# The last banks of pool, attention and two feed-forward layers finished by token tile, with the norm of tile 0 ahead of tile 1's statistics

## The chip, the core and the metric

The kernel runs on one core of a Trainium2 chip. Five engines work side by side, each with its own queue, and wait for each other by semaphores: TensorE (PE in the rows; PEld is its weight load), VectorE (DVE), ScalarE (ACT), GpSimd (POOL) and SyncE (SP, which here only issues transfers). The metric is the device time of one execution in microseconds.

## What is computed

The reference runs two blocks, one after the other, on a sequence of 256 tokens with 1024 features. The first has two mixers (mLSTM, gated linear attention), each followed by a mixture of 16 experts. The second, in which the change lies, is:

```python
def second_block(x, ...):
    for i in range(DEPTH):                       # 2
        if i % 2 == 0:
            h = _multiscale_pool(x, pool_w[j], pool_scale[j])
        else:
            h = _diff_attention(x, w_qkv[j], w_o[j], ...)
        x = _layernorm(ALPHA_2 * x + h, ln_mix_g[i], ln_mix_b[i])
        x = _layernorm(ALPHA_2 * x + _swiglu(x, w_gate[i], w_up[i], w_down[i]), ...)
    return x
```

So there are four layers, each closed by a layer norm: pool, feed-forward 0, attention, feed-forward 1. `_swiglu` is `(silu(x @ w_gate) * (x @ w_up)) @ w_down` with 2816 hidden features. The norm takes mean and variance over the 1024 features of a token. Everything is float32.

## The kernel before

Tokens lie in two tiles of 128 (i = 0, 1), features in two halves of 512 (c = 0, 1). The sum of a layer and its residual is gathered in four banks of the accumulation memory: `acc(i, c)` is bank 4 + 2i + c, so banks 4 and 5 are tile 0 and banks 6 and 7 are tile 1.

**Splits.** A product of the big layers is three matmuls on halves of a float32 number. For each chunk of weights ScalarE writes the high part (`w_hi`, line 563) and VectorE the rest (`w_lo`, line 568). TensorE waits for the rest by `split_ready`, and ScalarE may only write the next high part into a buffer when `chunk_done` says that TensorE is through with the chunk that lay there. `chunk_done` counts chunks, and TensorE raises it with the last matmul of a chunk.

**Feed-forward** (`ffn_tensor`). `down(s, at, units, base, end)` adds two chunks f = 0, 1 of the last product: for each f it waits for `split_ready` and for the hidden values (`fh_ready`), then runs banks 4, 5, 6, 7 with three matmuls each (line 1642). The last call has `end=True`. The high part of its chunk 1 can only be written when the chunk ahead in that buffer is done.

**Attention** (`att_tensor`). The output product runs over chunks 24 to 31 (`out_chunk`, matmuls at line 613). An even chunk adds to half 0 of both tiles (banks 4 and 6), an odd one to half 1 (banks 5 and 7). Its splits go through three buffers.

**Pool** (`pool_tensor`). Sixteen matmuls at line 1540, by group g of features and then by tile, so that the banks are finished in the order 4, 6, 5, 7.

**The norm.** `ln_statistics` (VectorE) waits for the banks in the order of `acc_waits`, takes `bn_stats` of each (line 331) and `bn_aggr` of a tile (line 334). ScalarE takes the root (`ln_scalar`, line 350), VectorE the reciprocal `rstd` and `nmr` (lines 323, 324), and then ScalarE writes half 0 of the normed rows `y` (line 353) and VectorE half 1 (line 344). TensorE transposes `y` (`transpose_x`, line 409), ScalarE scales it into `xT` (line 421), and VectorE splits that (lines 458, 460) for the next layer's matmuls. Ahead of each `transpose_x` but the first, `keep_clock(0, 10)` runs ten products of the identity with itself (line 392), whose results nobody reads. The last norm is `final_vector` (lines 369, 371), whose rows go out by four transfers of SyncE.

**What stands between on the queues.** Each queue is in order. At the end of feed-forward 0 and of attention ScalarE has first the high part of the next layer's chunk 0, which waits for `chunk_done` of all but the last chunk, then the table load and the roots of the norm. VectorE takes the rest of the next layer's chunks 0 and 1 right behind the last rows `y`, ahead of the split of `xT`.

## Time and profile before

| | us |
|---|---|
| median of three runs | 1791.68 |
| lowest, highest | 1790.61, 1797.0 |
| the profiled execution | 1799.73 |
| its span, first to last instruction | 1798.0 |
| TensorE busy in it | 1417.8 |
| VectorE busy | 600.7 |
| ScalarE busy | 426.8 |

The experts take the stretches up to about 1250 us, in which the core moves some 424 GB/s of weights. What the change touches lies behind that: the pool ends at 1274 us, feed-forward 0 at 1471 us, attention at 1591 us and feed-forward 1 at 1788 us of the span. Of a row of the timeline the first number is the start in us from the span's start, the second how long it took; a bracket at its end is the engine's idle time before it and what ended that. A row may hold several instructions (x8).

### The profile page before, as it was taken

Reading aid. Unit: us, or ns where it says so; the run is one execution under the profiler, and the core shown is the slowest. Engines: PE = TensorE matmul, PEld = TensorE weight load, DVE = VectorE, ACT = ScalarE, POOL = GpSimd, SP = SyncE. Lnnn points to the kernel's source line nnn. Section 1 sums busy time; section 2 is a strip of 40 time slices with the busy share of each in tenths; the row PEclk is TensorE's granted clock in tenths of the full one; section 3 lists DMA queues with packets and bytes.
Section 4 is the critical chain, followed back from the end, with each engine's and each line's share of the span. In section 5 each row is a group of like instructions: output and inputs, shape, how many; then the busy total and the mean of one; then the engine's idle time right before and its main releaser. Section 6 shows DMA issues by size and latency. Waiting matters only on the chain.

```text
span 1798.0 us, 21119 instructions
## 1 busy us (share of the span) xinstructions
PE 1417.8 (79%) x8842; PEld 914.0 (51%) x8842; DVE 600.7 (33%) x988; ACT 426.8 (24%) x671; POOL 39.5 (2%) x47
## 2 busy tenths in 40 slices
PE   7999765576575689987665655757999999999997
PEld 6787221121121275672211211212999989889996
DVE  5555100000000147651000000001555566865556
ACT  3442000000000143430000000001434454653443
POOL 3000000000000002100000000000000000000000
PEclk9988978787687889999776887877999999999999
DMA  9736999999999952369999999999365665226560
GB/s 338 215 115 262 379 423 424 423 424 425 423 424 424 397 202 94 128 270 392 424 424 424 424 424 424 424 424 395 131 201 186 211 219 179 71 94 193 183 207 23
DMA packets 145635, 533.47 MB, mean 297 GB/s; under 512 B 9740, under 2 KB 73500, under 8 KB 96284
## 3 DMA queue, kind: packets, MB, share of 16 engines
q1 hardware_dynamic: 142948, 527.07, 74.7%
q10 hardware_dynamic: 1176, 2.18, 0.8%
q0 software_dynamic: 1440, 3.18, 0.6%
q8 instruction: 55, 0.90, 0.2%
q14 instruction: 16, 0.13, 0.0%
HBM read 529.78 MB, written 2.62 MB: 296 GB/s over the span
## 4 chain that ended last, share of the span: by engine, by line
PE 52%; DMA 35%; DVE 5%; SPq 4%; ACT 2%; issue 1%; POOL 0%; DVEq 0%; ACTq 0%; POOLq 0%
PE bank L1626 14%; PE bank L613 11%; DMA moe_slots<-in_moe_w_up 7%; DMA arena<-in_moe_w_up 7%; PE bank L1642 7%; PE bank L1104 5%; DMA ring<-in_moe_w_down 4%; DMA ring<-in_moe_w_up 4%; SPq L1270 4%; DMA xT<-in_moe_w_down 3%; DMA moe_slots<-in_moe_w_down 3%; DMA xT<-in_moe_w_up 3%; PE bank L497 3%; PE bank L1143 3%; PE bank L1085 2%; DMA h_slot<-in_moe_w_up 2%
## 5 line engine op out<-in xcount | busy, mean ns | idle before, releaser
L568 DVE TENSOR_TENSOR w_lo<-ring,w_hi 128x1024 fp32r<-128x1024 f32 x200 | 244.3, 1224 | 238.0 <-ACT w_hi L563 230.9
L1104 PE MATMUL bank<-ring,arena 128*32 128x512 f32 x1016 | 214.9, 731 | 100.3 <-DMA ring<-in_moe_w_up 41.2
L563 ACT ACTIVATE w_hi<-ring 128x1024 fp32r<-128x1024 f32 x200 | 211.1, 1058 | 313.0 <-PE bank L1626 151.3
L1143 PE MATMUL bank<-ring,arena 128*32 128x512 f32 x536 | 158.2, 931 | 82.9 <-DMA arena<-in_moe_w_down 24.5
L1626 PE MATMUL bank<-xT_hi,w_hi 128*128 128x256 f32 x704 | 199.8, 284 | 0.6 <-DVE xT_lo L460 0.4
L1626 PE MATMUL bank<-xT_hi,w_lo 128*128 128x256 f32 x704 | 199.2, 283 | 0.0
L1626 PE MATMUL bank<-xT_lo,w_hi 128*128 128x256 f32 x704 | 199.2, 283 | 0.0
L1237 DVE TENSOR_TENSOR arena<-arena,bank 64x512 f32<-64x512 f32 x32 | 22.1, 691 | 450.1 <-ACT arena L1177 450.1
L1104 PEld LDWEIGHTS bank<-ring,arena 128*32 128x32 f32 x1016 | 46.9, 122 | 223.5 <-issue 206.3
L1626 PEld LDWEIGHTS bank<-xT_hi,w_hi 128*128 128x128 f32 x704 | 135.0, 192 | 1.6 <-issue 0.9
L1626 PEld LDWEIGHTS bank<-xT_lo,w_hi 128*128 128x128 f32 x704 | 135.1, 192 | 0.7
L1626 PEld LDWEIGHTS bank<-xT_hi,w_lo 128*128 128x128 f32 x704 | 135.1, 192 | 0.0
L1177 ACT ACTIVATE arena<-bank 64x512 f32<-64x512 f32 x32 | 18.8, 588 | 463.0 <-PE bank L1104 463.0
L1104 PE MATMUL bank<-arena 128*32 128x512 f32 x448 | 98.4, 697 | 36.3 <-DMA ring<-in_moe_w_up 23.1
L1143 PEld LDWEIGHTS bank<-ring,arena 128*32 128x32 f32 x536 | 36.9, 162 | 170.7 <-issue 170.7
L1243 DVE COPY arena<-bank 128x512 f32<-128x512 f32 x8 | 5.5, 691 | 326.4 <-PE bank L1143 326.4
L1104 PE MATMUL bank<-moe_slots,arena 128*32 128x512 f32 x384 | 87.9, 741 | 33.6 <-DMA xT<-in_moe_w_up 18.6
L1143 PE MATMUL bank<-arena 128*32 128x512 f32 x192 | 72.9, 934 | 28.5 <-DMA ring<-in_moe_w_down 28.5
L1143 PE MATMUL bank<-moe_slots,arena 128*32 128x512 f32 x192 | 72.5, 916 | 26.4 <-DMA xT<-in_moe_w_down 26.4
L1184 ACT ACTIVATE arena<-bank 128x512 f32<-128x512 f32 x8 | 4.8, 597 | 345.7 <-PE bank L1143 345.7
L613 PE MATMUL bank<-w_hi,xT_hi 128*128 128x512 f32 x176 | 70.5, 400 | 5.2 <-DVE xT_lo L460 4.2
L1642 PE MATMUL bank<-w_hi,h_hi 128*128 128x512 f32 x176 | 70.4, 400 | 0.0
(286 smaller groups left out, 2282.9 us busy)
## 6 DMA issues: line engine op xcount, KB each, us to landing
ring<-in_moe_w_gate SPq DMA_DIRECT2D x76, 1024.0 KB, 26.4
ring<-in_moe_w_down SPq DMA_DIRECT2D x67, 1024.0 KB, 27.1
ring<-in_moe_w_up SPq DMA_DIRECT2D x51, 1024.0 KB, 26.7
arena<-in_moe_w_up SPq DMA_DIRECT2D x28, 1024.0 KB, 26.8
arena<-in_moe_w_gate SPq DMA_DIRECT2D x28, 1024.0 KB, 26.5
moe_slots<-in_moe_w_up SPq DMA_DIRECT2D x24, 1024.0 KB, 27.1
moe_slots<-in_moe_w_gate SPq DMA_DIRECT2D x24, 1024.0 KB, 26.5
moe_slots<-in_moe_w_down SPq DMA_DIRECT2D x24, 1024.0 KB, 27.0
```

The lines of the kernel that those rows point to most:

```text
L497: last = nc.tensor.matmul(ps[bank][:, :], xT3[:, kk, i * P:(i + 1) * P], w[:, k, :], start=(kk == 0), stop=(kk == KD - 1))
L563: nc.scalar.activation(dst, raw, ACT.Copy).then_inc(hi_ready, 1)
L568: nc.vector.tensor_tensor(lo, raw, hi.bitcast(F32), ALU.subtract).then_inc(split_ready, 1)
L613: last = nc.tensor.matmul(dst, *(ops if weights_first else ops[::-1]), start=(start and p == 0), stop=(stop and p == 2))
L1085: last = nc.tensor.matmul(ps[B_GA[k // 4]][:, (k % 4) * P:(k % 4 + 1) * P], pair_cols(y3[:, i, :], k), pick[:, i, :], start=(i == 0), stop ...
L1104: last = nc.tensor.matmul(ps[B_GU[j % 2]][32 * c:32 * c + 32, :], xin[:, k, j * CAP:(j + 1) * CAP], w, start=(k == 0), stop=(k == KD - 1), ...
L1143: last = nc.tensor.matmul(ps[B_DN[c]][32 * j:32 * j + 32, :], hT[:, j // 2, at:at + CAP], slot(ud[j], 2)[:, f % 2, c * HALF:(c + 1) * HALF ...
L1177: nc.scalar.activation(silu[64:128, j % 2, :], ps[B_GU[j % 2]][0:64, :], ACT.Silu).then_inc(silu_ready, 1)
L1237: nc.vector.tensor_tensor(hmid[64 * (j % 2):64 * (j % 2) + 64, j // 2, :], silu[64:128, j % 2, :], ps[B_GU[j % 2]][64:128, :], ALU.mult).t ...
L1270: sp.dma_start(slots[u.slot], src[:, q, :]).then_inc(slot_landed[u.slot], 16)
L1626: last = nc.tensor.matmul(ps[2 * s + f][:, n * SEQ:(n + 1) * SEQ], w_parts[wp][:, buf, k * P:(k + 1) * P], (xT_hi3, xT_lo3)[xp][:, k, :], ...
L1642: last = nc.tensor.matmul(acc(i, c), h_parts[hp][:, 2 * s + f, i * P:(i + 1) * P], w_parts[wp][:, f, c * HALF:(c + 1) * HALF], start=False ...
```

## The change

`TILE_FIRST = (4, 5, 6, 7)` names the four norms of the second block. For these:

- TensorE ends with tile 0 first. The pool loops over tiles outside and groups inside. The last `down` of a feed-forward runs tile 0 of chunk 0, tile 0 of chunk 1, and then tile 1 of both; the waits for both chunks stand ahead of tile 1, and `chunk_done` of both is raised in tile 1's part. Attention runs tile 0 of chunks 30 and 31, then tile 1 of both, and raises `chunk_done` with tile 1 as well.
- VectorE takes tile 0's reciprocal and rows ahead of the wait for bank 7, where before it took the reciprocal there and the rows behind bank 7's statistics.
- `transpose_x` has no identity products ahead of tile 0's transposes and seven between tile 0's and tile 1's.

```diff
+        TILE_FIRST = (4, 5, 6, 7)
+        def xhat(dve, n, i):
+            dve.wait_ge(rstd_ready, NT * n + i + 1)
+            nc.vector.tensor_scalar(y3[:, i, HALF:D], acc(i, 1), rstd[:, i:i + 1], nmr[:, i:i + 1],
+                                    ALU.mult, ALU.add).then_inc(xhat_vec, 1)
...
             for at, (i, c, done, count) in enumerate(acc_waits()[n]):
+                if at == 3 and n in TILE_FIRST:
+                    inverse_std(0)
+                    rows(0)
                 dve.wait_ge(done, count)
-                if at == 3:
+                if at == 3 and n not in TILE_FIRST:
                     inverse_std(0)
...
         def transpose_x(pe, gen):
-            if gen:
+            if gen and gen - 1 not in TILE_FIRST:
                 keep_clock(0, 10)
...
+                elif i and gen - 1 in TILE_FIRST:
+                    keep_clock(0, 7, P)
...
-            for g in range(4):
-                for i in range(NT):
+            for i in range(NT):
+                for g in range(4):
...
+            def down_tile(s, f, i, units, end):
+                for c in range(2):
+                    for p, (wp, hp) in enumerate(PARTS):
+                        last = nc.tensor.matmul(acc(i, c), ...)
+                if i == NT - 1:
+                    last.then_inc(chunk_done, 1)
...
                 for f in range(2):
                     pe.wait_ge(split_ready, at + (f + 1))
                     pe.wait_ge(fh_ready, base + (f + 1))
+                    for i in range(1 if end else NT):
+                        down_tile(s, f, i, units, end)
+                if end:
+                    for f in range(2):
+                        down_tile(s, f, 1, units, end)
...
-            for c in range(29, 32):
-                att_mix.out_chunk(pe, c)
+            att_mix.out_chunk(pe, 29)
+            for i in range(NT):
+                for c in (30, 31):
+                    att_mix.out_chunk(pe, c, (i,))
```

TensorE, the last two chunks of a feed-forward, before: from the middle of chunk 0 to the middle of chunk 1 (line 1642; a wait in brackets).

```order
L1642 MATMUL bank5<-w_lo,h_hi 128x512
L1642 MATMUL bank6<-w_hi,h_hi 128x512
L1642 MATMUL bank6<-w_hi,h_lo 128x512
L1642 MATMUL bank6<-w_lo,h_hi 128x512
L1642 MATMUL bank7<-w_hi,h_hi 128x512
L1642 MATMUL bank7<-w_hi,h_lo 128x512
L1642 MATMUL bank7<-w_lo,h_hi 128x512
L1642 MATMUL bank4<-w_hi,h_hi 128x512 [waits fh_ready,split_ready]
```

The same place now (the matmul has moved to line 1652).

```order
L1652 MATMUL bank4<-w_hi,h_hi 128x512 [waits fh_ready,split_ready]
L1652 MATMUL bank4<-w_hi,h_lo 128x512
L1652 MATMUL bank4<-w_lo,h_hi 128x512
L1652 MATMUL bank5<-w_hi,h_hi 128x512
L1652 MATMUL bank5<-w_hi,h_lo 128x512
L1652 MATMUL bank5<-w_lo,h_hi 128x512
L1652 MATMUL bank4<-w_hi,h_hi 128x512 [waits fh_ready,split_ready]
```

The six matmuls on banks 6 and 7 that stood ahead of the second wait now stand behind it, after the six on banks 4 and 5 of chunk 1.

VectorE, the norm after attention, before.

```order
L331 BN_STATS stats<-bank4 128x6 [waits chunk_done]
L331 BN_STATS stats<-bank6 128x6 [waits chunk_done]
L331 BN_STATS stats<-bank5 128x6 [waits acc_done]
L334 BN_AGGR mv<-stats 128x2 [waits vec_chain]
L323 RECIPROCAL rstd<-std 128x1 [waits std_ready,chunk_done]
L324 SCALAR_TENSOR_TENSOR nmr<-mv,rstd 128x1 [waits vec_chain]
L331 BN_STATS stats<-bank7 128x6
L334 BN_AGGR mv<-stats 128x2 [waits vec_chain]
L344 TENSOR_SCALAR y<-bank5,rstd,nmr 128x512 [waits rstd_ready]
L323 RECIPROCAL rstd<-std 128x1 [waits std_ready]
```

And now.

```order
L341 BN_STATS stats<-bank4 128x6 [waits acc_done]
L341 BN_STATS stats<-bank5 128x6 [waits acc_done]
L344 BN_AGGR mv<-stats 128x2 [waits vec_chain]
L341 BN_STATS stats<-bank6 128x6 [waits chunk_done]
L330 RECIPROCAL rstd<-std 128x1 [waits std_ready]
L331 SCALAR_TENSOR_TENSOR nmr<-mv,rstd 128x1 [waits vec_chain]
L322 TENSOR_SCALAR y<-bank5,rstd,nmr 128x512 [waits rstd_ready]
L341 BN_STATS stats<-bank7 128x6 [waits chunk_done]
L344 BN_AGGR mv<-stats 128x2 [waits vec_chain]
L330 RECIPROCAL rstd<-std 128x1 [waits std_ready]
```

Tile 0's rows have moved ahead of bank 7's statistics, and the second reciprocal now stands right behind the second aggregate, where before the rows of tile 0 lay between them.

## Rows read from the trace of the kernel before

**Rows 1.** The page's TensorE clock in 40 slices of the span, tenths of full speed.

```profile
PEclk9988978787687889999776887877999999999999
```

**Rows 2.** Busy time of stretches: PE, PEld, DVE, ACT, POOL; granted clock; DMA share, GB/s.

```profile
668.20:670.50 2.30, 0.00 (x0) 0.00 (x0) 1.03 (x1) 2.28 (x4) 0.00 (x0) 1.00 0.75 290
671.00:674.40 3.40, 3.40 (x16) 2.99 (x15) 3.37 (x6) 0.70 (x1) 0.00 (x0) 0.51 0.02 5
1475.10:1477.40 2.30, 0.00 (x0) 0.01 (x1) 2.27 (x4) 2.30 (x6) 0.00 (x0) 1.00 0.00 0
1477.50:1483.00 5.50, 5.50 (x25) 4.52 (x26) 4.95 (x8) 4.30 (x6) 0.00 (x0) 1.00 0.18 52
```

**Rows 3.** The timeline where the pool ends: start us, us, engine, line, operation.

```profile
1266.62 7.07 PE L1540 MATMUL bank<-ring,arena 128*128 128x256 f32 x32
...
1272.87 0.70 DVE L331 BATCH_NORM_STATS2 stats<-bank 128x6 f32<-128x512 f32 x1 [1.89 <-PE bank L1540]
...
1273.60 0.21 DVE L334 BATCH_NORM_AGGREGATE mv<-stats 128x2 f32<-128x12 f32 x1
...
1274.24 0.16 DVE L323 RECIPROCAL rstd<-std 128x1 f32<-128x1 f32 x1 [0.43 <-ACT std L350]
...
1276.04 0.15 DVE L323 RECIPROCAL rstd<-std 128x1 f32<-128x1 f32 x1
...
1276.42 0.78 ACT L353 ACTIVATE y<-bank,nmr,rstd 128x512 f32<-128x512 f32 x1 [0.65 <-DVE nmr L324]
...
1277.25 1.09 PE L409 MATMUL bank<-cst,y 128*128 128x128 f32 x8 [0.42 <-ACT y L353]
```

**Rows 4.** The timeline where feed-forward 0 ends.

```profile
1465.17 0.39 PE L1642 MATMUL bank<-w_hi,h_hi 128*128 128x512 f32 x1
...
1466.52 1.23 DVE L568 TENSOR_TENSOR w_lo<-ring,w_hi 128x1024 fp32r<-128x1024 f32 x1 [0.48 <-ACT w_hi L563]
...
1467.92 0.40 PE L1642 MATMUL bank<-w_hi,h_hi 128*128 128x512 f32 x1
...
1468.18 1.06 ACT L563 ACTIVATE w_hi<-ring 128x1024 fp32r<-128x1024 f32 x1 [1.69 <-PE bank L1642]
...
1469.26 1.28 ACT L350 ACT_TABLE_LOAD   x1
...
1470.43 0.40 PE L1642 MATMUL bank<-w_lo,h_hi 128*128 128x512 f32 x1
...
1470.55 0.30 ACT L350 ACTIVATE std<-mv,cst 128x1 f32<-128x1 f32 x1
1470.66 2.40 PE L392 MATMUL bank<-cst 128*128 128x128 f32 x20
...
1473.13 0.81 DVE L344 TENSOR_SCALAR y<-bank,rstd,nmr 128x512 f32<-128x512 f32 x1
...
1473.86 2.35 DVE L568 TENSOR_TENSOR w_lo<-ring,w_hi 128x1024 fp32r<-128x1024 f32 x2
...
1477.42 0.47 PE L613 MATMUL bank<-w_hi,xT_hi 128*128 128x512 f32 x1 [2.36 <-DVE xT_lo L460]
```

**Rows 5.** The timeline where attention ends.

```profile
1588.01 2.06 DVE L331 BATCH_NORM_STATS2 stats<-bank 128x6 f32<-128x512 f32 x3 [2.35 <-PE bank L613]
...
1588.07 1.06 ACT L563 ACTIVATE w_hi<-ring 128x1024 fp32r<-128x1024 f32 x1 [3.85 <-PE bank L613]
...
1590.45 0.30 ACT L350 ACTIVATE std<-mv,cst 128x1 f32<-128x1 f32 x1
...
1593.03 0.81 DVE L344 TENSOR_SCALAR y<-bank,rstd,nmr 128x512 f32<-128x512 f32 x1
```

**Rows 6.** The timeline where feed-forward 1, and with it the kernel, ends.

```profile
1783.78 1.23 DVE L568 TENSOR_TENSOR w_lo<-ring,w_hi 128x1024 fp32r<-128x1024 f32 x1 [0.50 <-ACT w_hi L563]
...
1787.71 0.39 PE L1642 MATMUL bank<-w_lo,h_hi 128*128 128x512 f32 x1
...
1794.80 0.75 DVE L371 SCALAR_TENSOR_TENSOR arena<-y,rstd,arena 128x512 f32<-128x512 f32 x1
```

More of the change, by code:

```diff
@@ L359, in final_vector, with rows @@
         def final_vector(dve, link, n):
-            inverse_std = ln_statistics(dve, link, n)
-            dve.wait_ge(gb_in, 32)
-            for i in range(NT):
-                if i:
-                    inverse_std(i)
+            def rows(i):
+                if i == 0:
+                    dve.wait_ge(gb_in, 32)
                 dve.wait_ge(rstd_ready, NT * n + i + 1)
@@ L603, in lo, with products @@
                     split_lo(dve, self.raw(c), self.buffer(c), self.at + c)
-            def products(self, pe, c, todo, operand):
+            def products(self, pe, c, todo, operand, more=False):
                 pe.wait_ge(split_ready, self.at + c + 1)
@@ L1536, in pool_tensor @@
             w = slots[u.slot].rearrange("p (g k n) -> p g k n", g=4, k=2)
-            for g in range(4):
-                for i in range(NT):
+            for i in range(NT):
+                for g in range(4):
                     for k in range(2):
@@ L1632, in gate_up @@
                         last.then_inc(chunk_done, 1)
+            def down_tile(s, f, i, units, end):
+                for c in range(2):
+                    for p, (wp, hp) in enumerate(PARTS):
+                        last = nc.tensor.matmul(acc(i, c), h_parts[hp][:, 2 * s + f, i * P:(i + 1) * P],
+                                                w_parts[wp][:, f, c * HALF:(c + 1) * HALF],
+                                                start=False, stop=(end and f == 1 and p == 2))
+                        if f == 1 and i == 0 and c == 0 and p == 0:
+                            last.then_inc(unit_done, units)
+                        if end and f == 1 and p == 2 and (i, c) != (1, 1):
+                            last.then_inc(acc_done, 1)
+                if i == NT - 1:
+                    last.then_inc(chunk_done, 1)
             def down(s, at, units, base, end=False):
@@ L1804, in out_chunk @@
                                        False, 2 * b + k2 == KD - 1, False)
-                                      for i in range(NT) for k2 in range(2)], ("z", 2))
+                                      for i in tiles for k2 in range(2)], ("z", 2), more=tiles == (0,))
         att_mix = HeadMixer(att_u, 4, chunk0["att"])
```

41 lines of the change are left out of this document (16 added, 25 removed).

## Prediction

> **What bounds the kernel now.** I read the chain of work that ended last first: it is half TensorE, a third transfers, and the transfers all belong to the experts, ahead of 1250 us. From there on the chain runs over TensorE inside a layer and hands over at each norm to VectorE and ScalarE and back. So an edit at a layer's end counts one for one if it moves the first matmul of the next layer. The granted clock tells the same: it changes again and again in the first 28 slices and stands near full in the last twelve [rows 1]. Then I read the timeline at the four ends. After the pool the order is: last matmul, bank 7's statistics, rows of tile 1 at 1276.42, tile 1's transposes at 1277.25 [rows 3]. After feed-forward 0 it is: last matmul at 1470.43, rows of tile 1 at 1473.13, two rests `w_lo` for the next layer on VectorE, the split of `xT`, first product at 1477.42 [rows 4]. Attention ends in the same way, and there ScalarE is late as well: it waits for a chunk until 1588.07, then loads a table, and its root of tile 0 at 1590.45 is what VectorE's reciprocal waits for [rows 5]. The last norm ends with VectorE at 1795.55 (1794.80 + 0.75), and the rest of the span is a transfer [rows 6].
>
> The reader should see that tile 1's rows, not tile 0's, release the next layer everywhere. Doing tile 0 earlier helps only where it takes work out of the way between the last bank and tile 1's rows.
>
> **What an end costs in steps.** From bank statistics to the aggregate are 0.73 us (1272.87 to 1273.60), from there over ScalarE's root to the reciprocal 0.64 (to 1274.24), from a reciprocal to its rows 0.38 (1276.04 to 1276.42) [rows 3]. With the new order bank 7 reaches tile 1's rows in 0.73 + 0.64 + 0.38 = 1.75 us. Before, the root of tile 1 ran under tile 0's rows; now the round over ScalarE (0.64, where VectorE waits) lies open.
>
> **Pool: 0.65 us gained.** The 32 records of line 1540 take 7.07 us [rows 3], so each of the 16 matmuls takes 0.44. By tile, bank 6 is done after twelve, at 1271.9, and bank 7 after sixteen, at 1273.7 as before. Statistics of bank 6 at 1272.0, reciprocal at 1272.65 (tile 0's root is long there), tile 0's rows at 1273.05, so VectorE is free when bank 7 ends at 1273.75. Tile 1's rows start 1.75 later, at 1275.5, where before it was 1276.42: 0.9 earlier. TensorE: tile 0's transposes go at 1273.9 and take 1.1 [rows 3]; seven identity products are 14 records, and 20 take 2.40, so 1.6 us [rows 4]; tile 1's transposes start at 1276.6 and not at 1276.35, against 1277.25 before. Gain 0.65; bounds 0 (the rest hides it) and 0.9 (the identity products hide).
>
> **Feed-forward 0: 3.35 us lost.** Two waits that were covered are laid open. *The first is TensorE's.* Before, chunk 0's twelve matmuls started at 1465.17 and chunk 1's at 1467.92, 0.23 each, and the rest of chunk 1 was ready at 1466.52 + 1.23 = 1467.75 [rows 4]: just in time, with no slack. Now TensorE has six matmuls of tile 0 to do, is through at 1466.5 and waits until 1467.8. VectorE's rest follows ScalarE's high part, and that waits for the chunk ahead in the buffer, so nothing brings it forward. Tile 0's banks end when they did before; tile 1's twelve matmuls follow, the last at 1471.8 where it was 1470.43: 1.37 late. *The second is ScalarE's.* Its high part for the next layer waits for `chunk_done` of chunk 0, which was raised at the end of the first twelve (ScalarE at 1468.18) and is now raised six matmuls into tile 1's part, at 1470.8. Queued behind it are the table load and tile 0's root: 1470.9 + 1.08 + 1.29 puts the root at 1473.27, where it was 1470.55 [rows 4]. VectorE stands behind that root with the reciprocal, and behind the reciprocal stands bank 7. Reciprocal at 1473.65, tile 0's rows at 1474.05, bank 7's statistics 0.68 later at 1474.73 (the bank has been done since 1472.2, its last matmul's start and 0.4), tile 1's rows 1.75 later, at 1476.48: 3.35 after 1473.13. The two rests and the split follow on VectorE as before [rows 4], so the first product moves to 1480.8. Bounds: 1.4, if only TensorE's wait counted, and 3.5.
>
> **Attention: 2.0 us lost.** Here TensorE doesn't wait and ends when it did. But chunk 30 is through after 18 of the last 24 matmuls and not after 12, six times 0.23 = 1.36 later, so ScalarE's high part moves from 1588.07 to 1589.43 and the root from 1590.45 to 1591.8 [rows 5]. Reciprocal 1592.2, tile 0's rows 1592.6, bank 7's statistics 1593.27, tile 1's rows 1595.0, against 1593.03: 2.0, of which 1.36 is the high part and the rest the open round over ScalarE. Bounds 0.6 and 2.1. A transfer that SyncE may now issue one matmul group earlier gives nothing, since its reader ScalarE comes later.
>
> **Feed-forward 1: 1.85 us lost.** TensorE waits again, until 1783.78 + 1.23 = 1785.01 [rows 6], and ends 1.37 later. No high part stands ahead of the root, which is ready early. Its last matmul starts at 1787.71 + 1.37 = 1789.1, bank 6's last three before that and is done 0.4 after its start, at 1788.8, and VectorE waits for it: statistics 1788.8, reciprocal 1789.4, rows from 1789.8, four operations of 0.75 each [rows 6], a little overlapped, in 2.9, bank 7's statistics at 1792.7, then 0.73, 0.64 and 0.38, and four operations in 3.0: end at 1797.4, against 1795.55. Bounds 1.2 and 2.0.
>
> Sum: -0.65 + 3.35 + 2.0 + 1.85 = **+6.55 us**.
>
> **The clock.** Without identity products ahead of tile 0's transposes TensorE now stands still for 2.7 us after feed-forward 0 (1472.2 to 1474.9) and after attention (1590.7 to 1593.4); before, the products filled that. The rows show both outcomes for a still stretch of this size: after 2.3 us without a matmul at 668 us the granted clock was 0.51 in the next 3.4 us, after 2.3 us at 1475 us it stayed 1.00 [rows 2]. I counted eleven still stretches of 2.2 to 2.8 us that began at full clock, of which one of each kind stands in the rows; six were followed by a fall, so each of the two has about an even chance, and it may differ from run to run. A fall makes TensorE's 2.7 us of transposes and identity products take up to twice as long, 1.5 to 2.7 more; VectorE's two rests (2.3 us) hide some 0.3 to 0.8 of it. I take 1.3 us for a fall, with 0 and 3 as bounds (3 if it reaches the first products).
>
> The Trainium skill (TensorE: Matmul & The Clock Gate, "What's actually happening") says that the throttled state is the default and that activity releases it; that speaks against taking the identity products away, and by it both places fall and the time would be 1791.7 + 6.55 + 2.6 = 1800.8. The trace agrees only half, by the two stretches of [rows 2].
>
> **Rivals.** *Both falls or a long one.* Clock 0.5 after both ends, or into the first products: 6.55 + 2.6 to 6 = 9 to 12.5 us, 1801 to 1804. For it speaks the row at 671 us, against it the one at 1475 us [rows 2].
> *Faster: the waits don't bite.* The norm gives 0.65 after the pool and, since bank 7's way is 1.75 us and not 2.3, some 0.5 after each of feed-forward 0 and attention, 1.7 in all: 1790.0. It decides at the rest of the last chunk: it needs `w_lo` by 1466.5, and the trace has 1467.75, right when TensorE came for it; and it needs ScalarE's high part not to be last, where the trace has it ahead of the root at both ends [rows 4, 5]. So it has little behind it.
> *Half of it hides.* The late ends are met by slack that I don't see, for instance if the first layers' matmuls wait for something else anyway, or if the high part is in time: 1 to 5 us, 1792.7 to 1796.7. Against it: after feed-forward 0 the first product starts as soon as the split is there.
>
> **Numbers.** The profiled execution took 1799.73 us, 8.05 above the median, with the experts' transfers ahead of 1250 us in it; the edits lie behind and carry over to the median as differences. Likeliest is the sum with one fall, 6.55 + 1.3 = 7.85: 1791.68 + 7.85 = **1799.5 us** (1807.6 for an execution like the profiled one). Chances: the sum with none or one fall 0.58, both or a long fall 0.25, half hidden 0.12, faster 0.05. The range goes from 1795.5 (half hidden at its upper end) to 1803.0 (most of the long falls). About 0.5%, 9.0 us, is what a measurement of this kernel can tell from no change; my 7.85 is 0.44%, just inside it. Both falls or a long one, and the upper end of the first case, lie beyond it: slower 0.33, same 0.65, faster 0.02.
>
> **What would show it.** In the changed kernel's trace: a still TensorE of 1.3 us between the sixth and seventh of the last 24 matmuls of each feed-forward; tile 0's root 2.7 us later against the last matmul's old place after feed-forward 0, 1.4 later after attention; VectorE idle for 0.4 us between the second aggregate and reciprocal at all four; tile 1's rows 1.75 us after bank 7's statistics; after the pool first transposes of tile 1 0.65 earlier. Wrong would be: a rest of the last chunk that comes earlier than 1.3 us after TensorE is through with tile 0, or a root ahead of bank 6.

## The result, and the profile after

The changed kernel took **1801.71 us** (median of 8 runs, 1798.78 to 1803.77) and the kernel before 1792.51 (8 runs, 1790.61 to 1800.0): a ratio of **1.0042**, 95% interval 1.0025 to 1.0059. That is the ratio of the means, 1801.57 and 1794.05, so the loss is 7.5 us, with 4.5 to 10.6 us as its interval; the medians differ by 9.2. The forecast was 1799.5 us, 7.85 us lost. The ratios of the experiments are not the quotients of the medians beside them either. The profiled execution of after took 1803.34 us, its span 1801.6.

What lies ahead of the pool differs from one execution to the next: the pool's first matmul starts between 1258.1 and 1266.6 us of the span in the fourteen traces of this study, with nothing changed ahead of it. Small terms can't be read from the span or the time of one execution then. I count each station (a place in the program that every version passes) from the pool's first matmul and compare with the same distance in before. By that count the end of after is 7.85 us late, in one execution.

**The pool's end**, timeline of after; columns as in [rows 3].

```profile
1262.39 7.07 PE L1554 MATMUL bank<-ring,arena 128*128 128x256 f32 x32
...
1269.50 0.70 DVE L341 BATCH_NORM_STATS2 stats<-bank 128x6 f32<-128x512 f32 x1
...
1270.52 1.73 PE L403 MATMUL bank<-cst 128*128 128x128 f32 x14
1270.80 0.16 DVE L330 RECIPROCAL rstd<-std 128x1 f32<-128x1 f32 x1 [0.36 <-ACT std L358]
...
1271.19 0.78 ACT L361 ACTIVATE y<-bank,nmr,rstd 128x512 f32<-128x512 f32 x1 [0.42 <-DVE nmr L331]
...
1272.08 1.04 PE L422 MATMUL bank<-cst,y 128*128 128x128 f32 x8
```

Tile 1's rows start 8.80 us after the first matmul (1271.19 - 1262.39), where [rows 3] have 9.80 (1276.42 - 1266.62). The way from bank 7's statistics to the rows is 1.69 us, with VectorE idle for 0.36 behind ScalarE's root. Tile 1's transposes start 0.11 us after ScalarE has written the rows (1271.19 + 0.78), so the seven identity products in front of them cost next to nothing. Two things make up the gain. From bank 7's statistics to the rows before needs 1.91 us (1276.42 less the first row below), 0.22 more than now. And its statistics stood behind the reciprocal of tile 0, which waited for ScalarE's root: they start 7.89 us after the first matmul, now 7.11. Timeline of before, bank 7's statistics behind the pool, feed-forward 0 and attention, with attention's last matmul:

```profile
1274.51 0.69 DVE L331 BATCH_NORM_STATS2 stats<-bank 128x6 f32<-128x512 f32 x1
...
1471.22 0.69 DVE L331 BATCH_NORM_STATS2 stats<-bank 128x6 f32<-128x512 f32 x1
...
1590.31 0.40 PE L613 MATMUL bank<-w_lo,xT_hi 128*128 128x512 f32 x1
...
1591.12 0.69 DVE L331 BATCH_NORM_STATS2 stats<-bank 128x6 f32<-128x512 f32 x1
```

**Feed-forward 0's end**, timeline of after, to be laid beside [rows 4].

```profile
1462.62 0.50 PE L1652 MATMUL bank<-w_hi,h_hi 128*128 128x512 f32 x1 [1.09 <-DVE w_lo L581]
...
1465.73 1.06 ACT L576 ACTIVATE w_hi<-ring 128x1024 fp32r<-128x1024 f32 x1 [4.42 <-PE bank L1652]
...
1466.60 0.39 PE L1652 MATMUL bank<-w_lo,h_hi 128*128 128x512 f32 x1
1466.81 1.28 ACT L358 ACT_TABLE_LOAD   x1
1468.10 0.30 ACT L358 ACTIVATE std<-mv,cst 128x1 f32<-128x1 f32 x1
1468.43 0.16 DVE L330 RECIPROCAL rstd<-std 128x1 f32<-128x1 f32 x1 [1.38 <-ACT std L358]
...
1469.55 0.69 DVE L341 BATCH_NORM_STATS2 stats<-bank 128x6 f32<-128x512 f32 x1
...
1469.66 1.09 PE L422 MATMUL bank<-cst,y 128*128 128x128 f32 x8 [2.67 <-ACT y L361]
...
1471.24 0.81 DVE L322 TENSOR_SCALAR y<-bank,rstd,nmr 128x512 f32<-128x512 f32 x1
...
1475.52 0.76 PE L626 MATMUL bank<-w_hi,xT_hi 128*128 128x512 f32 x1 [2.33 <-DVE xT_lo L473]
```

The chain can be read downwards: TensorE has done its six matmuls of tile 0 and waits 1.09 us for the rest of the last chunk (first row), ScalarE has waited 4.42 us for a bank before it may write the next layer's high part, then come the table load and the root, VectorE's reciprocal has waited 1.38 us for that root, and TensorE stands still for 2.67 us until ScalarE has written tile 0's rows. The page "ScalarE: Activation LUTs" of the Trainium skill (section "What ACT_TABLE_LOAD costs") has 1283 ns for the load, as the row shows, and a drain of 1380 ns on top; here the root starts 0.01 us behind the load, so the row decides and a switch costs this queue 1.3 us.

**The clock behind it**, stretches of after; columns as in [rows 2].

```profile
1470.80:1473.20 2.40, 2.39 (x22) 2.15 (x20) 2.29 (x5) 1.98 (x4) 0.00 (x0) 1.00 0.00 0
1473.20:1475.50 2.30, 0.00 (x0) 0.01 (x1) 2.27 (x4) 2.30 (x6) 0.00 (x0) 1.00 0.00 0
1475.60:1478.90 3.30, 3.30 (x8) 2.62 (x9) 2.86 (x6) 3.27 (x5) 0.00 (x0) 0.50 0.00 0
1479.00:1483.00 4.00, 4.00 (x19) 3.28 (x18) 2.45 (x2) 1.12 (x2) 0.00 (x0) 1.00 0.37 100
```

The identity products and tile 1's transposes (first row) have the full clock. Attention's first products run at 1.2 GHz (granted clock 0.50) for 3.3 us: 8 matmuls where the next stretch has 19 in 4.0 us at 2.4 GHz. In [rows 2] the same products have the full clock from their start.

**Attention's end**, timeline of after, beside [rows 5].

```profile
1589.12 1.06 ACT L576 ACTIVATE w_hi<-ring 128x1024 fp32r<-128x1024 f32 x1 [5.22 <-PE bank L626]
...
1589.99 0.39 PE L626 MATMUL bank<-w_lo,xT_hi 128*128 128x512 f32 x1
...
1590.19 1.28 ACT L358 ACT_TABLE_LOAD   x1
...
1591.49 0.30 ACT L358 ACTIVATE std<-mv,cst 128x1 f32<-128x1 f32 x1
1591.82 0.16 DVE L330 RECIPROCAL rstd<-std 128x1 f32<-128x1 f32 x1 [2.02 <-ACT std L358]
...
1592.94 0.69 DVE L341 BATCH_NORM_STATS2 stats<-bank 128x6 f32<-128x512 f32 x1
...
1594.62 0.81 DVE L322 TENSOR_SCALAR y<-bank,rstd,nmr 128x512 f32<-128x512 f32 x1
```

The last matmul starts at 1589.99, so tile 1's rows come 4.63 us behind it; in before 2.72 (1593.03 - 1590.31). VectorE waits 2.02 us for the root. The root starts 1.50 us behind the last matmul here and behind feed-forward 0 alike, where in before it was 0.14 (1590.45 - 1590.31) and 0.12 us (1470.55 - 1470.43).

**Feed-forward 1's end**, timeline of after, beside [rows 6].

```profile
1785.48 1.23 DVE L581 TENSOR_TENSOR w_lo<-ring,w_hi 128x1024 fp32r<-128x1024 f32 x1 [0.49 <-ACT w_hi L576]
...
1786.76 0.50 PE L1652 MATMUL bank<-w_hi,h_hi 128*128 128x512 f32 x1 [1.08 <-DVE w_lo L581]
...
1790.52 0.70 DVE L341 BATCH_NORM_STATS2 stats<-bank 128x6 f32<-128x512 f32 x1 [1.12 <-PE bank L1652]
...
1790.77 0.39 PE L1652 MATMUL bank<-w_lo,h_hi 128*128 128x512 f32 x1
...
1795.79 0.16 DVE L330 RECIPROCAL rstd<-std 128x1 f32<-128x1 f32 x1 [0.36 <-ACT std L388]
...
1798.41 0.75 DVE L378 SCALAR_TENSOR_TENSOR arena<-y,rstd,arena 128x512 f32<-128x512 f32 x1
```

TensorE has done its six matmuls of tile 0 and waits 1.08 us for the rest of the last chunk. Its last matmul is 8.39 us ahead of VectorE's end (1799.16), in before 7.84 (1795.55 - 1787.71).

### The profile page after: what moved, and what is told of

It is laid out like the page before. It is cut to its first block, busy times and chain, and to the rows that moved or that the text cites. A ratio compares the mean times of both kernels' runs of the same rounds, so it can differ in the third digit from the quotient of the medians.

```text
span 1801.6 us, 21081 instructions
## 1 busy us (share of the span) xinstructions
PE 1404.4 (78%) x8824; PEld 907.8 (50%) x8824; DVE 601.7 (33%) x988; ACT 427.2 (24%) x671; POOL 39.4 (2%) x47
## 4 chain that ended last, share of the span: by engine, by line
PE 49%; DMA 40%; DVE 5%; SPq 3%; ACT 2%; issue 1%; POOL 0%; ACTq 0%; DVEq 0%; POOLq 0%
PE bank L1640 14%; PE bank L626 11%; DMA moe_slots<-in_moe_w_up 7%; DMA arena<-in_moe_w_up 7%; PE bank L1652 7%; DMA ring<-in_moe_w_up 6%; DMA xT<-in_moe_w_down 4%; DMA ring<-in_moe_w_down 4%; PE bank L1118 3%; DMA h_slot<-in_moe_w_up 3%; DMA moe_slots<-in_moe_w_down 3%; DMA xT<-in_moe_w_up 3%; PE bank L510 3%; PE bank L1157 3%; SPq L1278 2%; DMA h_slot<-in_moe_w_down 2%
## 5 line engine op out<-in xcount | busy, mean ns | idle before, releaser
L1118 PE MATMUL bank<-ring,arena 128*32 128x512 f32 x1016 | 210.8, 718 | 102.2 <-DMA ring<-in_moe_w_up 41.3
L1157 PE MATMUL bank<-ring,arena 128*32 128x512 f32 x536 | 148.6, 877 | 87.0 <-DMA moe_slots<-in_moe_w_down 25.7
L1118 PE MATMUL bank<-arena 128*32 128x512 f32 x448 | 97.6, 719 | 38.9 <-DMA ring<-in_moe_w_up 19.5
L1118 PE MATMUL bank<-moe_slots,arena 128*32 128x512 f32 x384 | 87.0, 739 | 36.3 <-DMA moe_slots<-in_moe_w_up 18.5
L1157 PE MATMUL bank<-arena 128*32 128x512 f32 x192 | 68.2, 890 | 27.4 <-DMA ring<-in_moe_w_down 27.4
L1157 PE MATMUL bank<-moe_slots,arena 128*32 128x512 f32 x192 | 69.3, 877 | 24.6 <-DMA xT<-in_moe_w_down 24.6
```

The source lines that it names most:

```text
L1118: last = nc.tensor.matmul(ps[B_GU[j % 2]][32 * c:32 * c + 32, :], xin[:, k, j * CAP:(j + 1) * CAP], w, start=(k == 0), stop=(k == KD - 1), ...
L1157: last = nc.tensor.matmul(ps[B_DN[c]][32 * j:32 * j + 32, :], hT[:, j // 2, at:at + CAP], slot(ud[j], 2)[:, f % 2, c * HALF:(c + 1) * HALF ...
```

## The stations of all runs

Each row of the table is one profiled execution. The first column is the start of the pool's first matmul in the span. The others are the station's start counted from there, minus the same of before: ff0, ff1 are the feed-forwards, att is attention, "rows" is the start of tile 1's `y`, "first" a layer's first product, "end" the end of VectorE's last operation. The last column is a fall of the granted clock behind the pool and ahead of the last matmul: where it began, and how long it lasted.

| | pool first | ff0 first | ff0 last matmul | rows | att first | att last matmul | rows | ff1 first | ff1 last matmul | end | fall (for) |
|---|---|---|---|---|---|---|---|---|---|---|---|
| before | 1266.62 | 0 | 0 | 0 | 0 | 0 | 0 | 0 | 0 | 0 | none |
| c1_before | 1260.44 | 0.01 | 0.33 | 0.31 | 0.32 | 0.32 | 0.33 | 0.33 | 0.61 | 0.61 | none |
| after | 1262.39 | -0.99 | 0.41 | 2.33 | 2.33 | 3.92 | 5.83 | 5.83 | 7.29 | 7.85 | 1475.5 (3.4) |
| c2_after | 1263.47 | -0.98 | 0.72 | 2.65 | 3.29 | 3.26 | 5.17 | 5.17 | 6.90 | 7.47 | 1472.4 (3.4) |
| c3_after | 1264.33 | -0.99 | 0.37 | 2.30 | 3.10 | 3.07 | 4.98 | 4.98 | 6.32 | 6.89 | 1472.8 (3.4) |
| e1_pool_only | 1260.38 | -0.99 | -0.92 | -0.91 | -0.92 | -0.92 | -0.93 | -0.93 | -0.85 | -0.87 | none |
| e2_down_old | 1261.13 | -0.99 | -1.00 | -0.43 | -0.43 | -0.44 | 1.48 | 1.47 | 1.50 | 2.19 | none |
| e3_ident | 1263.85 | -0.99 | 0.36 | 2.29 | 2.28 | 2.24 | 4.16 | 4.16 | 5.44 | 6.00 | none |
| e4_act_queue | 1263.29 | -0.99 | 0.44 | 0.89 | 0.88 | 2.46 | 2.26 | 2.25 | 3.70 | 4.27 | 1475.3 (3.4) |
| e6_best | 1258.12 | -0.99 | -1.01 | -1.01 | -1.01 | -1.03 | -1.24 | -0.37 | -0.40 | -0.39 | none |
| e7_three_held | 1260.14 | -0.99 | -0.31 | 1.62 | 1.62 | 1.57 | 3.48 | 4.38 | 5.06 | 5.62 | 1588.2 (3.4) |
| e8_queues | 1261.12 | -0.99 | -0.75 | -0.78 | -1.41 | -0.79 | -0.99 | -0.12 | 0.13 | 0.14 | none |
| e9_down_only | 1261.83 | -0.99 | 0.73 | 2.11 | 2.11 | 4.84 | 4.84 | 4.84 | 6.44 | 6.40 | 1473.8 (6.8) |
| e10_kept | 1261.57 | -0.99 | -0.68 | -0.70 | -0.70 | 0.81 | 0.61 | 0.61 | 0.86 | 0.88 | 1471.5 (3.4) |

Up to 0.3 us of a difference comes in each feed-forward's body, without any edit (c1_before), so a term below 0.3 is not resolved by one trace. Differences between two stations of one layer's end are steadier: rows behind attention's last matmul are 1.91 late in after, c2_after and c3_after alike. The times have a scatter of their own: the median of before was 1792.51, 1796.02, 1796.41 and 1796.78 us in the four series, so a kernel is compared only with the before of its own series.

## The experiments

**The kernels of the record again: c1_before, c2_after, c3_after.** No edit. They ask whether terms and falls repeat.

> The kernel before, once more, to see how far its own stretches and its clock differ between executions. My account: every milestone counted from the pool's first matmul within 0.1 us of the first profile at full clock; if the clock falls after feed-forward 0 in the still stretch of 2.3 us ahead of attention's first product, attention is 1.6 us or more longer here too.

> The changed kernel, once more. My account: 6.3 us over before from the pool on where the clock holds, 7.9 where it falls once; every other milestone within 0.1 us of its first profile. Rival (the fall belongs to the change): it falls again in the same place after feed-forward 0.

> The changed kernel a third time, for the same question: 6.3 us over before from the pool on with the clock at full, 1.6 more for each fall.

Measured: one time each, 1794.16, 1804.08 and 1804.33 us. Terms repeat within 0.3 us and not within the 0.1 that was expected (feed-forward 0's last matmul 0.33 late in c1_before, and in c2_after 0.31 later than in after). The fall came behind feed-forward 0 in all three traces of after and in none of before; behind attention in none. But it lay elsewhere. In c2_after the granted clock fell while TensorE was on the identity products and tile 1's transposes:

```profile
1469.10:1472.30 3.20, 1.25 (x11) 1.25 (x12) 2.01 (x6) 1.76 (x4) 0.00 (x0) 1.00 0.15 44
1472.50:1475.70 3.20, 3.20 (x17) 3.20 (x17) 3.16 (x4) 2.21 (x4) 0.00 (x0) 0.50 0.00 0
```

These are stretches of c2_after. Seen from tile 1's rows the first product is then 0.64 us late (3.29 - 2.65), 0.80 in c3_after; where the fall reached the products instead (after), it took 1.59 (3.92 - 2.33). VectorE's rests hide part of the first kind and nothing of the second.

**e1_pool_only: the pool's part alone.**

```diff
-        TILE_FIRST = (4, 5, 6, 7)
+        TILE_FIRST = (4,)
```

and `down`, attention and their norms in their old order.

> Only the pool and its norm go by tile; attention and both feed-forward layers are as in the kernel before, the ten identity products ahead of their transposes too. My account (each end is a sum of its own): from the pool's first matmul to the first product of feed-forward 0 1.0 us less than before (0.99 in the changed kernel's trace), every later stretch as before within 0.2 us, the whole 1.0 us faster, 1791.5. Rival (the late ends come from something that the four ends share, such as the clock after the pool): feed-forward 0 and attention would still come 2 to 4 us late. After feed-forward 0 TensorE stands still 2.3 us as before; if the clock falls there with no other edit, the fall in the changed kernel was not the edit's alone, and the first products of attention take some 1.6 us more.

Measured: 1795.0 us (10 runs) beside 1796.02 (23); ratio 1.0002, 0.9992 to 1.0011. The trace is 0.99 early at the first product of feed-forward 0 and 0.87 at the end. So the gain is there in the trace and 0.87 of it arrives at the end, and it is too small for the times: 0.9 us is 0.0005, and the interval holds that as well as nothing.

**e2_down_old: after, with the old order of the last `down`.**

```diff
-                    for i in range(1 if end else NT):
+                    for i in range(NT):
                         down_tile(s, f, i, units, end)
-                if end:
-                    for f in range(2):
-                        down_tile(s, f, 1, units, end)
```

> The changed kernel, with one part undone: the last down of both feed-forward layers runs all banks of chunk 0, then all banks of chunk 1, as before; the order of the norms, of attention and of the pool and the identity products stay changed. My account (TensorE's bare wait for the last rest, and chunk_done raised late, cost the feed-forward ends; the norm's new order costs only the open round over ScalarE): last matmul of feed-forward 0 where it was before, tile 1's rows 0.6 late and not 3.3, the kernel's end 0.7 late after feed-forward 1 and not 2.0; 4.0 us less than the changed kernel in all, about 2.3 over the kernel before at full clock, plus 1.6 where the clock falls. Rival (the norm's order is what costs): tile 1's rows stay over 2 us late with the old matmul order.

Measured: 1798.05 us (10 runs), ratio 1.0012 (0.9997 to 1.0027). Feed-forward 0's end costs 0.56 (-0.99 to -0.43) and not 3.32, that of feed-forward 1 0.72 (1.47 to 2.19) and not 2.02, attention's 1.92 as in after. So 2.8 and 1.3 us go with the order of the matmuls. The last matmul comes when it did before, and what is left behind it, 0.57 (-1.00 to -0.43), is the norm's new order alone. Timeline of e2_down_old, feed-forward 0's last matmul and bank 7's statistics:

```profile
1463.94 0.39 PE L1652 MATMUL bank<-w_lo,h_hi 128*128 128x512 f32 x1
...
1465.53 0.69 DVE L341 BATCH_NORM_STATS2 stats<-bank 128x6 f32<-128x512 f32 x1
```

The statistics start 1.59 us behind the last matmul, where in before it was 0.79 (1471.22 - 1470.43): tile 0's rows, 0.8 us, now stand ahead of them. From there the rows are 1.69 us away and not 1.91, so 0.22 of it comes back. This trace shows no fall.

**e9_down_only: the opposite, `TILE_FIRST = (4,)` and attention's old order, but the new order of `down`.**

> The kernel before with the pool by tile and one more part of the change alone: the matmul order of the last down of both feed-forward layers, with the norms in the old order and the identity products where they were. My account: TensorE ends 1.36 late at both, the root after feed-forward 0 is 2.7 late by chunk_done, tile 1's rows there 2.7 late (0.6 less than with the norm's new order), the end of the kernel 1.3 late at feed-forward 1. Rival (the norm's order is needed for the loss): under 1 us late at each.

Measured: one time, 1801.37 us. The rows behind feed-forward 0 are 3.10 late (-0.99 to 2.11; 2.7 were expected), since the last matmul is 1.72 late and not 1.4, as in c2_after. From feed-forward 0's last matmul to the rows it is 1.38 longer than in before (0.73 to 2.11), which is the late high part by itself, since the norm has its old order. With e2_down_old's 0.57 that makes 1.95, where after has 1.92 (0.41 to 2.33): the two add up. At the kernel's end there is no high part, and the way from the last matmul to the end is that of before (6.44 to 6.40); the 1.60 lost there are TensorE's wait and the body.

The clock brought something new. This kernel has the ten identity products ahead of the transposes, as before has them, and yet a fall of 6.8 us, the longest of all. Stretches of e9_down_only:

```profile
1472.50:1474.70 2.20, 0.00 (x0) 0.00 (x0) 2.17 (x4) 2.20 (x6) 0.00 (x0) 0.79 0.00 0
1474.80:1480.50 5.70, 5.70 (x14) 4.44 (x15) 4.11 (x7) 3.58 (x6) 0.00 (x0) 0.50 0.00 0
```

It cost 2.73 us (2.11 to 4.84).

**e3_ident: after, with the ten identity products back behind feed-forward 0 and attention.**

```diff
-            if gen and gen - 1 not in TILE_FIRST:
+            if gen and gen - 1 != 4:
```

> The changed kernel with the ten identity products back ahead of tile 0's transposes after feed-forward 0 and after attention (the seven between the tiles stay). My account, as predicted: with TensorE kept busy there the clock does not fall, the first products of attention run at full pace, and the whole is 1.6 us less than the changed kernel's profile, some 6.3 over before, with tile 1's rows where they are in the changed kernel. Rival (the fall comes from the second still stretch, ahead of attention's first product, which the kernel before has too, 2.36 us): the clock can fall here as well, and the products put back gain nothing.

Measured: 1803.21 us (5 runs), ratio 1.0042 (1.0025 to 1.0059), the same as after. Its one trace has no fall, as the account said, and ends 6.00 late where after's three have 6.9 to 7.9. But nothing of the 1.6 us expected stands in the times, and one trace without a fall is no proof that the products keep it away (e9_down_only). The terms at the ends are those of after (3.28, 1.92, 1.84), so the products cost nothing there.

**e4_act_queue: after, with the next layer's first high part between tile 0's and tile 1's root on ScalarE.**

```diff
-        def ln_scalar(act, n):
+        def ln_scalar(act, n, between=lambda: None):
             for i in range(NT):
+                if i:
+                    between()
...
-            att_mix.hi(act, 0)
-            ln_scalar(act, 5)
+            ln_scalar(act, 5, lambda: att_mix.hi(act, 0))
...
-            ffn_first_hi(act, 1, (0,))
-            ln_scalar(act, 6)
+            ln_scalar(act, 6, lambda: ffn_first_hi(act, 1, (0,)))
```

> The changed kernel with ScalarE's queue in another order at two places: the high part of the next layer's chunk 0 no longer stands ahead of the table load and tile 0's root but between tile 0's rows and tile 1's root. My account (the late chunk_done costs through ScalarE's queue): tile 0's root follows its aggregate at once; tile 1's rows after feed-forward 0 1.9 late against before and not 3.3, after attention 0.1 early and not 1.9 late; 3.4 us less than the changed kernel in all, 2.9 over before at full clock. Rival (VectorE or TensorE is the bound, and the root's lateness hides): under 0.5 us less at each end.

Measured: 1800.67 us (7 runs, 1797.23 to 1815.62), ratio 1.0037 (1.0006 to 1.0067); the one run at 1815.62 makes the interval wide, and the times don't tell this kernel from after. Timeline of e4_act_queue at feed-forward 0's end:

```profile
1466.22 0.29 ACT L360 ACTIVATE std<-mv,cst 128x1 f32<-128x1 f32 x1 [2.68 <-DVE mv L344]
...
1467.54 0.39 PE L1654 MATMUL bank<-w_lo,h_hi 128*128 128x512 f32 x1
1467.90 0.14 DVE L330 RECIPROCAL rstd<-std 128x1 f32<-128x1 f32 x1
...
1470.69 0.81 DVE L322 TENSOR_SCALAR y<-bank,rstd,nmr 128x512 f32<-128x512 f32 x1
```

The root is ahead of the last matmul now, and the reciprocal has no wait in its row. The end of feed-forward 0 costs 1.88 (-0.99 to 0.89) and not 3.32, attention's -0.20 (2.46 to 2.26) and not 1.91. So the queue behind `chunk_done` was 1.4 us of the one and all of the other (2.1). The last matmul of feed-forward 0 is as late as in after: its 1.4 us are TensorE's own wait. This trace shows the fall again, 1.58 (0.88 to 2.46).

**e7_three_held: after, with nine matmuls of chunk 0 ahead of the wait for chunk 1 and not six** (banks 4, 5 and 6; bank 7's three come behind tile 0 of chunk 1).

```diff
                     for i in range(1 if end else NT):
                         down_tile(s, f, i, units, end)
+                    if end and f == 0:
+                        down_tile(s, 0, 1, units, end, (0,))
                 if end:
-                    for f in range(2):
-                        down_tile(s, f, 1, units, end)
+                    down_tile(s, 0, 1, units, end, (1,))
+                    down_tile(s, 1, 1, units, end)
```

> The changed kernel, with half of the held-back matmuls in both last downs: of chunk 0 banks 4, 5 and 6 run ahead of the wait for chunk 1, and only bank 7's three follow tile 0 of chunk 1. My account (TensorE waits for the last rest as long as it has no matmuls to run, 0.23 us each, and chunk_done comes as much later): TensorE ends 0.7 us late after each feed-forward and not 1.36, tile 1's rows after feed-forward 0 come 2.6 us late and not 3.3, the end after feed-forward 1 is 0.7 less than in the changed kernel. Rival (the wait is for something else and its length does not follow the number of matmuls): the same 1.36 and 3.3.

Measured: one time, 1798.87 us. The last matmul is 0.68 late (-0.99 to -0.31), where after has 1.40 and e2_down_old nothing: with 0.23 us each, three matmuls held back are 0.69 and six 1.38. The rows are 2.61 late (-0.99 to 1.62), 0.7 less than in after, and feed-forward 1's end costs 1.24 (4.38 to 5.62), 0.8 less. Here the fall came behind attention, the only one there, and cost 0.90 (3.48 to 4.38).

**e6_best: what the runs had spoken for.** `TILE_FIRST = (4, 6)`, `down` in its old order, attention in the new one with e4_act_queue's order on ScalarE, and ten identity products ahead of the transposes behind both.

> What the runs so far leave of the change: the pool by tile (0.95 us less than before) and attention by tile with ScalarE's next high part behind tile 0's rows (0.2 less there), both feed-forward ends as before, the ten identity products ahead of all but feed-forward 0's transposes. Counted from the pool's first matmul to the end: 1.15 us less than before at full clock, 1791.4 in all. Rival (the ends are not independent, a stretch that is shortened gives its gain back in the next): 0.3 less or nothing.

Measured: 1795.8 us (10 runs) beside 1796.41 (19); ratio 1.0002 (0.9988 to 1.0015). The rows behind attention are 0.21 early (-1.03 to -1.24), but ff1's first product is 0.87 late against them, and the end is 0.39 early where 1.15 was expected. Timeline of e6_best:

```profile
1583.24 1.04 PE L426 MATMUL bank<-cst,y 128*128 128x128 f32 x8
1583.29 0.78 ACT L363 ACTIVATE y<-bank,nmr,rstd 128x512 f32<-128x512 f32 x1 [0.42 <-DVE nmr L331]
...
1584.11 1.73 PE L407 MATMUL bank<-cst 128*128 128x128 f32 x14
1585.67 1.04 PE L426 MATMUL bank<-cst,y 128*128 128x128 f32 x8
```

Tile 1's rows are written at 1584.1, but the seven identity products start just then, since the ten ahead had kept TensorE from tile 0's transposes until 1583.24. Its transposes follow 2.38 behind the rows' start, in after 0.91. Both sets of products are too many as soon as the rows come early.

**e10_kept: e6_best without the ten products behind attention.**

```diff
-            if gen and gen - 1 != 4:
+            if gen and gen - 1 not in TILE_FIRST:
```

> The kernel of the kept parts (pool and attention by tile, ScalarE's next high part behind tile 0's rows after attention, both feed-forward ends as before) without the ten identity products ahead of tile 0's transposes after attention; the seven between the tiles stay. My account (the sixteen or so products that stood there were now longer than tile 1's way and put its transposes 1.1 us late): the first product of feed-forward 1 comes as early as tile 1's rows, 1.2 us before the kernel before, and so the end; in the times, whose runs differ by more than that, no difference that can be told. Rival (something else holds tile 1's transposes): 0.4 us as in the run with the ten products.

Measured: 1793.79 us (12 runs, 1789.87 to 1795.55) beside 1796.78 (17 runs, 1791.91 to 1799.87); ratio **0.9982** (0.9973 to 0.9991), the only kernel that is faster than before. The lag behind attention is gone (0.61 at the rows and at the first product), as expected; that it would show in the times was not. But its trace shows a gain of 0.99 at the pool and 0.20 behind attention, and a fall of 1.51 in it (-0.70 to 0.81) with feed-forward 0's end built as in before: 0.88 late at the end. By the stations 1.2 us at most are explained, the interval asks for 1.6 to 4.9. The traces show nothing for the rest. It is one series, and e6_best, which the stations put 0.87 us away, has a ratio of 1.0002; so that e10_kept is faster is measured once, and why stays open.

**e8_queues: e6_best, with the high part and the rest of the next layer's second block of weights moved back** (ScalarE and VectorE): behind the first part of `xT` for attention, behind all of it for feed-forward 1.

```diff
-            att_mix.hi(act, 1)
-            xT_scalar(act, 6)
+            xT_scalar(act, 6, lambda: att_mix.hi(act, 1))
```

and the like on VectorE and behind attention.

> The kernel of the kept parts (pool and attention by tile), with the next layer's second chunk moved behind on ScalarE and VectorE after feed-forward 0 and after attention: its high part and its rest come after the first pair of xT (attention) or after all of xT (feed-forward 1), where before they stood between tile 1's rows and the first split. My account (VectorE's two rests, 2.3 us, are what releases the first product there): one rest leaves the path, the first product comes 0.7 to 0.9 us earlier at each of the two, 1.6 us in all, 2.7 less than before from the pool on. Rival (the root and transposes are as late as the rests): under 0.3 us at each, or a loss when the second chunk is then late for TensorE.

Measured: 1797.07 us (10 runs), ratio 1.0003 (0.9989 to 1.0018). Attention's first product comes 0.63 earlier than the rows' shift (-0.78 to -1.41), and the last matmul has it back (-0.79): the splits on VectorE are as much work as before, and the products wait for them later. Behind attention nothing moved: the first product is 0.87 late against the rows (-0.99 to -0.12), exactly as in e6_best, whose ten products are here too. So of the 1.6 us expected 0.63 came, at one of two places, and it didn't last: an earlier first product is no gain where the layer behind it waits for its splits later.

## Why the prediction was right, and where it was not

**Which row releases the next layer** held: without a fall in between, the first product moved with tile 1's rows in each trace, except in e6_best and e8_queues, whose edits changed what stands between the two. The way from bank 7's statistics to the rows is 1.68 to 1.70 us at all four ends where 1.75 was worked out. The other signs are there too: TensorE waits between the sixth and seventh of the last 24 matmuls (1.09 and 1.08 us in the rows, where 1.3 was named), tile 0's root comes 1.38 and 1.36 us later behind the last matmul (1.50 us against 0.12 and 0.14), and VectorE is idle for 0.36 us behind each second aggregate.

**One cause was misread.** The prediction puts part of each loss to the round over ScalarE that the new order lays open. But in before the way from bank 7's statistics to the rows is 1.91 us (1274.51 to 1276.42, 1471.22 to 1473.13, 1591.12 to 1593.03), so the new way is 0.22 shorter, open round and all. What the new order of the norm costs behind feed-forward 0 and attention is that tile 0's rows, 0.8 us, stand ahead of bank 7's statistics. The sums were right since they went by the order of the operations, in which those rows stand.

**Pool: mis-sized.** 0.99 gained, forecast 0.65, bounds 0 and 0.9. It is above the upper bound. The step that failed is the one on TensorE: it put 1.1 us for tile 0's transposes and 1.6 for the products in a row behind bank 7's end, and had tile 1's transposes wait 0.25 for them. From start to start the two groups take 0.93 and 1.56 (1269.59 is where tile 0's transposes begin, 7.20 behind the first matmul), because the recorded durations of neighbouring groups overlap. So TensorE is through 9.69 us behind the first matmul, 0.11 after the rows are written, and the rows themselves come 0.1 earlier than worked out, by a round that takes 0.57 from aggregate to reciprocal (1270.23 to 1270.80) and not 0.64. The rows' whole gain arrives.

**Feed-forward 0: right in size and in parts.** 3.32 lost (3.35). TensorE's wait makes the last matmul 1.35 to 1.43 us late in four of the six traces with the new `down` and all six matmuls held back (1.37); in c2_after and e9_down_only it is 1.70 and 1.72, with 0.3 from the layer's body. Six matmuls held back make that, three 0.68 (e7_three_held), none nothing (e2_down_old). The high part behind `chunk_done` makes 1.38 of the rest (e9_down_only; e4_act_queue gives 1.44 back), the new order of the norm 0.57 (e2_down_old). 1.37 + 1.38 + 0.57 is 3.32.

**Attention: right in size, not in its parts.** 1.91 lost (2.0). ScalarE's queue was named as 1.36 of it and the open round as the rest; e4_act_queue gives back 2.1. With the root early, bank 7's statistics start 0.83 us behind the last matmul (0.81 in before, 2.95 in after), so tile 0's rows fit in ahead of them, and the shorter way leaves a gain of 0.20 (0.20 and 0.21 in e10_kept and e6_best too). The same order on ScalarE leaves 0.45 lost behind feed-forward 0's last matmul (0.44 to 0.89). Attention finishes bank 6 six matmuls ahead of bank 7, a feed-forward three: in e4_act_queue bank 6's statistics start 0.84 us ahead of attention's last matmul and 0.25 ahead of feed-forward 0's. I read the difference from that, but no run changed it alone.

**Feed-forward 1: right.** 2.02, 2.30 and 1.91 in the three traces of after (1.85, bounds 1.2 and 2.0, so two lie above; the body of the layer adds up to 0.3 by itself). In e2_down_old, without TensorE's wait, 0.72 is left, nearly all of it behind the last matmul (1.50 to 2.19): 0.36 is VectorE's idle time behind tile 1's aggregate, which before doesn't have there; the rest wasn't taken apart.

**The clock: the size was near, the reason only half right.** One fall was forecast for 1.3 us, and the three traces have one each, of 1.59, 0.64 and 0.80. The prediction laid it to the missing identity products, with an even chance at each of two ends. In c2_after and c3_after it did begin behind the 2.7 us still stretch that was named (1.2 to 1.4 us after TensorE had gone to work again), in after behind the next one, of 2.33 us ahead of attention's first product, which before has too [rows 2]. Over all fourteen traces, an end without the ten products ahead had a fall in 5 of 13 cases (4 of 6 behind feed-forward 0, 1 of 7 behind attention), an end with them in 2 of 15 (e9_down_only and e10_kept, behind feed-forward 0). That leans the way the prediction had it, but it is few cases, the products don't prevent a fall, and the times of e3_ident, which has them, are those of after. So the cause of a fall is not settled, and "an even chance at each end" is not borne out for attention.

Counted by still stretches instead of ends it looks different again. Stretches of 2.7 us that the change makes ahead of tile 0's transposes stand nine times in these traces, and three were followed by a fall (c2_after, c3_after, e7_three_held). The one of 2.3 to 2.4 us ahead of attention's first product, which before has as well, stands eleven times and began at full clock, and four were followed by a fall (after, e4_act_queue, e9_down_only, e10_kept). So the stretch that was there already took the clock about as often as the new one, and taking the products away mainly adds a second place where it can happen. In e2_down_old and e4_act_queue the first stretch behind feed-forward 0 is so short that it doesn't count here, though the products are gone.

By the rule of the Trainium skill that the prediction cited (TensorE: Matmul & The Clock Gate, "What's actually happening"), the throttled state is the default and comes back without activity. The traces agree as far as each fall stands behind a still stretch, and not with what was made of it: two falls, where each trace has one. The 1800.8 us that went with it can't be told from the forecast by the times, whose median is 1801.71.

**The sum** agrees to the last digit by luck. -0.99 + 3.32 + 1.59 + 1.91 + 2.02 is 7.85, the forecast; but a pool 0.34 better and a fall 0.29 dearer cancel, and c3_after has 6.89 for the same code. The loss in the times, 7.5 us, has an interval of 4.5 to 10.6, which would fit none as well as two falls.

**The rivals.** "The waits don't bite" fell with the first wait at either feed-forward. Its gain of 0.5 at each norm also rested on a wrong reading, 2.3 us for the old way of bank 7 where the trace has 1.91; what is left is the 0.20 behind attention. "Both falls or a long one" appeared in none of after's traces; e9_down_only shows that a long one exists. "Half of it hides" would have had its place at the ends, and nothing hid there.

## What to carry to other kernels

Before an order of work is changed so that one half ends early, look at who else reads the same counter: here a "chunk done" raised six matmuls later held ScalarE's queue, and with it the root of the half that was meant to be early, for 1.4 us. Ending by tile pays only where all operands are there and no queue is late (the pool, 0.99 gained, and attention, 0.20 once ScalarE's root is early); where the last chunk arrives just in time, each matmul held back behind it is paid in full. The second tile's rows release the next layer, so whatever of the first tile is put ahead of the second's statistics must be done before these could start anyway. Small terms are to be counted between stations of one trace, and a version is kept by its times.

## What the runs showed of the hardware

The same code behind the same still stretch of TensorE kept its full clock in one execution and fell to 1.2 GHz in another. Stretches of e10_kept, in which feed-forward 0 ends as in before:

```profile
1469.40:1471.60 2.20, 0.00 (x0) 0.00 (x0) 2.17 (x4) 2.20 (x6) 0.00 (x0) 0.97 0.00 0
1471.70:1474.80 3.10, 3.10 (x8) 2.42 (x9) 2.91 (x6) 3.07 (x5) 0.00 (x0) 0.50 0.00 0
```

Beside it [rows 2] have 2.3 us without a matmul and 1.00 behind. The kernel of after itself shows both: behind its 2.67 us stretch after feed-forward 0 the granted clock stayed 1.00 in after and fell in c2_after and c3_after. What a fall costs depends on what lies under it: 0.64 to 0.90 us under transposes beside VectorE's rests, 1.51 to 1.59 in the first products, 2.73 where it lasted 6.8 us. Identity products ahead of the first transposes did not prevent it, though ten of them and the sixteen transposes kept TensorE at work until 2.2 us (e10_kept) and 1.4 us (e9_down_only) ahead of the fall.
